# Bf16 three-part expert adds, one pair behind, and expert weights loaded by halves of the partitions

## The reference

```python
comb = jnp.sum(jax.nn.one_hot(eid, N_EXPERTS, dtype=F32) * (gw[:, None] * top_p)[..., None], axis=1)
a = jnp.einsum("nd,edf->nef", hf, w_gate)
u = jnp.einsum("nd,edf->nef", hf, w_up)
hid = jax.nn.silu(a) * u * comb[..., None].astype(h.dtype)
return jnp.einsum("nef,efd->nd", hid, w_down).reshape(B, T, D)
```

## Time and profile before

| | us |
|---|---|
| median of 3 runs | 1246.7 (1243.45 to 1247.94) |
| the profiled execution, its own time | 1241.49 |
| its span | 1239.8 |
| PE busy | 1141.6 (92%) |
| DVE busy | 470.2 (38%) |
| ACT busy | 233.4 (19%) |
| expert stage, layer 0 | about 347 to 629 |
| expert stage, layer 1 | about 928 to 1224 |

### The profile page before, as it was taken

The page is one execution under the profiler, slowest core; times in us unless marked ns, Lnnn a source line. Parts: engine busy times, 40 slices in busy tenths (PEclk is TensorE's granted clock), DMA queues, the critical chain, the costliest instruction groups (busy, mean ns, idle before and its releaser), DMA issues.

```text
span 1239.8 us, 13174 instructions
## 1 busy us (share of the span) xinstructions
PE 1141.6 (92%) x4522; PEld 491.0 (40%) x4522; DVE 470.2 (38%) x1089; ACT 233.4 (19%) x433; POOL 95.8 (8%) x163
## 2 busy tenths in 40 slices
PE   4899999999689999999959999999969999999984
PEld 0444444445333333333334554544633333333332
DVE  0453232336722333333364232235672333333335
ACT  0523220302310000000024233332330000000003
POOL 4000000004210000000040000001320000000000
PEclk8999999999799999999979999999779999999998
DMA  9966548427959999999650421212656999999962
GB/s 376 382 255 257 201 190 345 186 113 271 389 183 415 379 385 393 380 383 385 250 204 35 153 79 66 94 42 77 228 197 268 407 379 382 385 387 383 390 229 90
DMA packets 51241, 328.32 MB, mean 265 GB/s; under 512 B 6145, under 2 KB 8785, under 8 KB 14465
## 3 DMA queue, kind: packets, MB, share of 16 engines
q1 hardware_dynamic: 44672, 299.92, 61.5%
q0 software_dynamic: 4912, 20.95, 4.5%
q10 hardware_dynamic: 1616, 6.93, 1.5%
HBM read 320.90 MB, written 6.88 MB: 264 GB/s over the span
## 4 chain that ended last, share of the span: by engine, by line
PE 82%; DMA 8%; DVE 5%; ACT 2%; issue 2%; SPq 1%; DVEq 0%; ACTq 0%; PEldq 0%
PE bank L654 35%; PE bank L1029 17%; PE bank L1055 13%; PE bank L1046 9%; DMA ring<-in_w_moe 3%; PE bank L675 3%; DMA ring<-in_w_mod 2%; DMA ring<-in_w_out 1%; PE bank L1038 1%; PE bank L1071 1%; DMA ring<-in_w_in 1%; DMA region<-h_store,toki 1%; PE bank L1091 1%; PE bank L1012 1%; ACT hT L1410 1%
## 5 line engine op out<-in xcount | busy, mean ns | idle before, releaser
L1029 PE MATMUL bank<-ring,region 128*64 128x512 f32 x1024 | 237.6, 608 | 5.9 <-issue 5.9
L1055 PE MATMUL bank<-region 128*128 128x512 f32 x384 | 173.3, 601 | 0.0
L654 PE MATMUL bank<-ring,hT 128*128 128x512 f32 x384 | 171.6, 599 | 1.6 <-DMA ring<-in_w_in 1.6
L1029 PEld LDWEIGHTS bank<-ring,region 128*64 128x64 f32 x1024 | 70.2, 138 | 148.1 <-issue 148.1
L1046 PE MATMUL bank<-ring,region 128*64 128x512 f32 x512 | 115.8, 594 | 4.9 <-DMA ring<-in_w_moe 2.9
L1055 PEld LDWEIGHTS bank<-region 128*128 128x128 f32 x384 | 70.3, 190 | 102.5 <-issue 102.5
L654 PEld LDWEIGHTS bank<-ring,hT 128*128 128x128 f32 x384 | 70.9, 190 | 90.4 <-issue 90.2
L2079 DVE TENSOR_TENSOR region<-bank,region 128x512 f32<-128x512 f32 x128 | 82.4, 686 | 42.8 <-PE bank L1046 42.8
L654 PE MATMUL bank<-ring,region 128*128 128x512 f32 x192 | 86.4, 599 | 4.4 <-ACT region L1506 1.6
L654 PE MATMUL bank<-hT,ring 128*128 128x384 f32 x256 | 89.2, 500 | 1.1 <-DMA ring<-in_w_in 1.1
L2075 DVE TENSOR_TENSOR region<-region,bank 128x256 f32<-128x256 f32 x32 | 13.5, 422 | 200.9 <-ACT region L1535 200.9
(11 more groups left out here) (302 smaller groups left out, 970.3 us busy)
## 6 DMA issues: line engine op xcount, KB each, us to landing
ring<-in_w_moe SPq DMA_DIRECT2D x201, 1024.0 KB, 8.5
ring<-in_w_mod SPq DMA_DIRECT2D x48, 1024.0 KB, 9.7
ring<-in_w_in SPq DMA_DIRECT2D x24, 1024.0 KB, 8.2
ring<-in_w_out SPq DMA_DIRECT2D x4, 1024.0 KB, 7.3
ring<-in_w_out SPq DMA_DIRECT2D x8, 512.0 KB, 6.9
region<-gate_store POOLq DMA_DIRECT2D x4, 1024.0 KB, 6.6
region<-in_lnrows POOLq DMA_DIRECT2D x4, 1024.0 KB, 8.5
h_store<-region ACTq DMA_DIRECT2D x6, 512.0 KB, 3.0
```

What stands on the lines that cost most here:

```text
L654: ins = pe.matmul(out, lhsT, rhs, start=start, stop=stop, skip_group_check=True)
L1029: ins = pe.matmul(bank[6][u * CAP:(u + 1) * CAP, :], xs[:, k, u * CAP:(u + 1) * CAP], ring[:, u, j, at:at + 2 * DE], start=k == 0, stop=k ...
L1055: ins = pe.matmul(bank[2 * t + y][:, :], cwp[:, t * P:(t + 1) * P], ysb[:, min(t, 1), y * HALF:(y + 1) * HALF], start=False, stop=False, s ...
```

## The change

Four things are altered together.

1. **The add of the two latent blocks is in bf16, in three parts.** Every row has one token and thus one latent weight. `pair_weights` now also sums the latent part of `cwp` over the row into `wlat`; `gated` multiplies the latent copy by `wlat` and the gate row in one instruction; `cut_y` (DVE) and `cut_rows` (ACT) cut that f32 row into three bf16 rows, `hi`, `mid` and `lo`, by rounding and subtracting twice; `onehot` is a bf16 0/1 matrix out of `cwp > 0`. `add_parts` multiplies `onehot` by each of the three parts. The context block stays one f32 matmul with `cwc`, a copy of the context part of `cwp`.
2. **The add stands one pair behind.** In the loop PE runs up_first(i), turn(i-1), up_second(i), add(i-2), down(i-1); after the loop add(14) follows down(15), and add(15) is the old f32 `add_pair` on `ylast`. `cw_ready` is now given at the end of `cut_y`. 
3. **The halves of `down` change banks**: half 0 goes to bank 6 and half 1 to bank 7, and the wait for `hid_ready` of the next pair moves ahead of both. `up_first` waits for `ya_sb` instead of `yb_sb`, `turn_step` for `yb_sb` instead of `ya_sb`.
4. **The expert weights lie by partition in HBM and in the ring.** `w_moe` becomes (6, 128, 32 x 2048), the ring (128, 3, 2, 2048). `bring(i, y, j)` loads piece j of both experts of the pair for 64 of the 128 partitions, 16 KB in a row, so there are still two requests of 1 MB for a piece, and each consumer waits for both as before. In HBM the rows of one request are 256 KB apart. The last pair's down weights and the extra turns are still 128 partitions with 8 KB.

The core of the diff:

```diff
-                def bring(i, u, j):
-                    sp.dma_start(ring[:, u, j, :], A["w_moe"][bass.ds((l * NE + G * i + u) * 3 + j, 1)].rearrange("a p n -> p (a n)"))\
-                      .then_inc(landed[u][j], 16)
+                def bring(i, y, j):
+
+                    r = slice(y * P // 2, (y + 1) * P // 2)
+                    sp.dma_start(ring[r, j, :, :].rearrange("p g n -> p (g n)"), A["w_moe"][l * 3 + j, r, bass.ds(i * (G * PIECE), G * PIECE)])\
+                      .then_inc(landed[y][j], 16)
...
+            def add_parts(sig):
+
+                for y in range(2):
+                    c = slice(y * HALF, (y + 1) * HALF)
+                    for t in (1, 2):
+                        for part in (hi, mid, lo):
+                            pe.matmul(bank[2 * t + y][:, :], onehot[:, (t - 1) * P:t * P], part[:, c], start=False, stop=False, skip_group_check=True)
+                    ins = pe.matmul(bank[y][:, :], cwc, ysb[:, 0, c], start=False, stop=False, skip_group_check=True)
                 ins.then_inc(sig, 1)
...
                 up_first(1)
                 up_second(1)
-                add_step(0)
                 with pe.Fori(2, NPAIR) as i:
                     up_first(i)
                     turn_step(i - 1)
                     up_second(i)
+                    add_step(i - 2)
                     down_step(i - 1)
-                    add_step(i - 1)
...
-                down_step(NPAIR - 1, last=True)
-                add_step(NPAIR - 1, last=True)
+                down_step(NPAIR - 1, last=True)
+                add_step(NPAIR - 2)
+                add_pair((S["ya_sb"], S["yb_sb"]), NPAIR + p0, S["comb_done"])
...
+                def cut_rows(i):
...
+                    for y in range(2):
+                        c = slice(y * HALF, (y + 1) * HALF)
+                        act.wait_ge(S[("ya_sb", "yb_sb")[y]], i + (p0 + 1))
+                        f(hi[:, c], ysb[:, 1, c], ACT.Copy).then_inc(S["y_cut"], 1)
+                    for y in range(2):
+                        c = slice(y * HALF, (y + 1) * HALF)
+                        act.wait_ge(S["y_rest"], i * 2 + (2 * l * (NPAIR - 1) + y + 1))
+                        f(mid[:, c], ysb[:, 1, c], ACT.Copy).then_inc(S["y_cut"], 1)
...
+                def cut_y(i):
+                    c0 = l * (NPAIR - 1)
+                    dve.tensor_scalar(onehot, cwp[:, P:N], 0.0, None, ALU.is_gt)
+                    dve.tensor_copy(cwc, cwp[:, 0:P])
+                    for y in range(2):
+                        c = slice(y * HALF, (y + 1) * HALF)
+                        dve.wait_ge(S["y_cut"], i * 4 + (4 * c0 + y + 1))
+                        dve.tensor_tensor(ysb[:, 1, c], ysb[:, 1, c], hi[:, c], ALU.subtract).then_inc(S["y_rest"], 1)
+                    pair_weights(i + 1)
+                    for y in range(2):
+                        c = slice(y * HALF, (y + 1) * HALF)
+                        dve.wait_ge(S["y_cut"], i * 4 + (4 * c0 + y + 3))
+                        ins = dve.tensor_tensor(lo[:, c], ysb[:, 1, c], mid[:, c], ALU.subtract)
+                    ins.then_inc(S["cw_ready"], 1)
```

More of the change, by code:

```diff
@@ L333, in backbone_step @@
         xrows = [htok[:, t, :] for t in range(NT)] + [ysb[:, s, :] for s in range(2)] + [xlast]
+        bf = lambda a: a.bitcast(BF16)
+        hi, mid, lo = bf(htok[:, 0, 0:HALF]), bf(htok[:, 0, HALF:D]), bf(htok[:, 1, 0:HALF])
+        onehot = bf(htok[:, 1, HALF:HALF + N_LAT // 2])
+        cwc = htok[:, 1, HALF + P:HALF + 2 * P]
+        wlat = htok[:, 1, HALF + 2 * P:HALF + 2 * P + 1]
+        ylast = (xlast, htok[:, 2, :])
         xrow = [hT[0:MAXL, 2 + i, 0:MAXJ * NE].rearrange("p (a b) -> p a b", a=MAXJ) for i in range(5)]
@@ L1129, in down_step, with add_step @@
                             pe.wait_ge(landed[u][2], at(i))
-                    down(0, S["ya_ready"], 0 if last else 2)
                     if not (last or isinstance(i, int) and i == 0):
                         pe.wait_ge(S["hid_ready"], i + (p0 + 2))
+                    down(0, S["ya_ready"], 0 if last else 2)
                     down(1, S["yb_ready"], 0 if last else 2)
-                def add_step(i, last=False):
-                    pe.wait_ge(S["cw_ready"], i + (p0 + 1))
-                    add_pair((S["ya_sb"], S["yb_sb"]), i + (p0 + 1), S["comb_done"])
-                    if not last:
-                        pe.sem_inc(used[2], G)
+                def add_step(i):
+                    pe.wait_ge(S["cw_ready"], i + (l * (NPAIR - 1) + 1))
+                    add_parts(S["comb_done"])
+                    pe.sem_inc(used[2], G)
                 up_first(0)
@@ L2077, in gated @@
                 def gated(b, y):
-                    for s in (1, 0):
-                        ins = dve.tensor_tensor(ysb[:, s, y * HALF:(y + 1) * HALF], b, gate_row[:, s, y * HALF:(y + 1) * HALF], ALU.mult)
-                    return ins
+                    c = slice(y * HALF, (y + 1) * HALF)
+                    dve.scalar_tensor_tensor(out=ysb[:, 1, c], in0=b, scalar=wlat, in1=gate_row[:, 1, c], op0=ALU.mult, op1=ALU.mult)
+                    return dve.tensor_tensor(ysb[:, 0, c], b, gate_row[:, 0, c], ALU.mult)
@@ L2082, in keep_y @@
                 def keep_y(i):
+                    first = isinstance(i, int) and i == 0
+                    dve.wait_ge(S["cw_step"], i * 5 + 5 * (p0 + 1))
                     dve.wait_ge(S["ya_ready"], i + (p0 + 1))
-                    if not (isinstance(i, int) and p0 + i == 0):
+                    if not first:
                         dve.wait_ge(S["comb_done"], i + p0)
-                    gated(bank[7][:, :], 0).then_inc(S["ya_sb"], 1)
+                    gated(bank[6][:, :], 0).then_inc(S["ya_sb"], 1)
@@ L2090, in weights, with keep_last_y @@
+                def keep_last_y():
+                    for y, (got, done) in enumerate((("ya_ready", "ya_sb"), ("yb_ready", "yb_sb"))):
+                        c = slice(y * HALF, (y + 1) * HALF)
+                        dve.wait_ge(S[got], p0 + NPAIR)
+                        for s in (1, 0):
+                            ins = dve.tensor_tensor(ylast[s][:, c], bank[6 + y][:, :], gate_row[:, s, c], ALU.mult)
+                        ins.then_inc(S[done], 1)
                 def weights(col, step, done):
@@ L2100, in pair_weights @@
                 def pair_weights(i):
-                    if not (isinstance(i, int) and p0 + i == 0):
-                        dve.wait_ge(S["comb_done"], i + p0)
-                    weights(colq[:, bass.ds(i, 1)], S["cw_step"], i * 3 + 3 * p0).then_inc(S["cw_ready"], 1)
+                    done = i * 5 + 5 * p0
+                    weights(colq[:, bass.ds(i, 1)], S["cw_step"], done).then_inc(S["cw_step"], 1)
+                    dve.wait_ge(S["cw_step"], done + 4)
+                    dve.tensor_reduce(wlat, cwp[:, P:N], AX, ALU.add).then_inc(S["cw_step"], 1)
                 dve.wait_ge(S["xg_ready"], l + 1)
```

63 lines of the change are left out of this document (35 added, 28 removed).

## The result

The changed kernel takes 1653.68 us (median of 4, 1641.71 to 1654.98) against 1247.32 (1243.45 to 1250.43) for the kernel before: a ratio of 1.3261, with a 95% interval of 1.3226 to 1.3297. The profiled execution took 1653.11 us, its span is 1651.4. I had given 1237 with a range of 1230 to 1285, so the forecast was wrong; of the rivals, the whole of rival 2 (half the partitions as a narrow door, 1615, a chance of 0.14) came true.

What follows compares the result with a forecast made beforehand. The loop was taken as PE-bound with at most 1.5 us of DMA room a pair. Per layer -2.4 - 12 x (16.32 - 15.6) + 6.5 = -4.5 us, two layers -9 from 1246.7: 1237 us, range 1230 to 1285.

Steps and rivals of the forecast that it cites:

- rival 2: Expert-weight requests filling 64 partitions fall toward 212 GB/s: 29.7 us a pair, near 1615 us; chance 0.14 for the whole.
- The rate of requests: Expert-weight loads in the loop: shrunken windows still fit, 403 GB/s at 15.6 us a pair; bounds 425 and 212.
- a part of the loss: Engines partly colliding on half-partition requests, for example 350 GB/s and 18.0 us a pair: 1260 to 1330 us, chance 0.10.
- The adds: PE's add in the expert loop: bf16 matmuls take half an f32 instruction's time, 4.46 us a pair instead of 5.35.
- rival 3: A bf16 matmul in the add is no shorter than an f32 instruction: 18.1 us a pair, 1297 us; chance 0.04.
- PE's work and the pair: Expert loop: 15.43 us of PE work a pair, taken as 15.6 with request jitter, from 16.32; ends 15.43 and 16.0.
- DVE: DVE's chain from the end of down to cw_ready: 7.0 us, done 0.5 us before PE reaches the add at 7.5.
- Rival 4: DVE is late, 8 us to cw_ready: 15.9 us a pair, 1244 us; chance 0.22 shared with the request-rate rival.
- Ahead of the loop: First pairs of a layer: add(0) leaves, request landings pace the ups, next up_first comes 2.4 us earlier.
- Behind the loop: From the end of up_second(15) to the last add: 25.0 us instead of 18.5, so 6.5 lost a layer.
- The stages outside: Stages outside the experts run the same instructions, so no time was put on them.
- The sum: Each layer: -2.4 ahead, 12 turns shortened from 16.32 to 15.6, +6.5 behind, -4.5 us; two layers -9 us.

Runs made afterwards that it cites:

- adds_only: Kernel before with only the adds changed, its requests and HBM layout kept: 1249.97 us, ratio 1.0038 to the kernel before.
- full128_rows8k: Changed kernel with its new HBM layout, each request bringing one expert on all 128 partitions in 8 KB rows: 1246.78 us, ratio 1.0014 to the kernel before.
- one_2mb_rows16k: Changed kernel with one 2 MB request per piece, both experts on 128 partitions in 16 KB rows: 1247.35 us, ratio 1.0030 to the kernel before.
- early_requests: full128_rows8k with the first requests of a layer asked for slot by slot, as in the kernel before: 1244.38 us, ratio 0.9993.
- middle_half: Changed kernel with each piece cut into one 1 MB request for partitions 32 to 95 and two of 0.5 MB for the rest: 1536.8 us.

## Why the prediction was wrong, step by step

**The rate of requests: the step that failed.** The sum's pair of 15.6 us stands on 403 GB/s, and the runs showed 215. The prediction took its rate terms of 392 to 425 GB/s from rows on 128 partitions, and wrote beside them that no row shows whether 64 partitions are slower. The forecast then carried the good end, with the queue's depth as its reason ("engines have room to be at different requests"). That reason was worth nothing: the rate was 215 with 19.6 us from a request to its landing, and 222 with two queues. Why the halves do not overlap, no run shows. The other end of the same sentence, 212, was right to 1.5%. Rival 2's working gave a pair of 29.7 us, measured 29.34, and 165 us a layer for the 12 turns and the ends, with some 20 more for the pairs at both ends, 185; measured 192.7 and 192.4. The other 27 us of the 412, the 22.0 and 4.6 that lie ahead of the pairs, it left out: above all the gather, from 9.10 to 27.39 us. The Trainium skill's rule in SBUF — State Buffer, "Door 1: The DMA port swizzle", gives 64 partitions 196 GB/s at 1 MiB and about 218 as the limit (215 measured here). It was the only evidence on the very operation that the change introduces, and it got 0.14, with 0.10 more for a part of the loss. Where the trace is silent on an operation and a rule speaks, the silence is no counterweight.

The rest of the steps can be judged in adds_only and full128_rows8k, where the rate is whole. One turn of adds_only:

```profile
399.86 3.63 PE bank L1037 x16
403.49 0.37 PE bank L1046 x2
403.86 3.58 PE bank L1037 x16
407.44 1.40 PE bank L1073 x6
408.84 0.86 PE bank L1074 x2
409.70 1.29 PE bank L1073 x6
411.00 0.86 PE bank L1074 x2
411.85 3.58 PE bank L1054 x16
415.44 3.63 PE bank L1037 x16
```

**The adds: right.** 1.40 + 0.86 + 1.29 + 0.86 = 4.41 us, predicted 4.46. Six bf16 matmuls take 1.29 to 1.40 us, 0.215 to 0.233 each, and two f32 instructions 0.43 each. Half the time for bf16 was right, and rival 3 falls.

**PE's work and the pair: nearly right.** A turn without a wait is 15.58 us (399.86 to 415.44), predicted 15.43. Twelve turns, 399.86 to 589.61, average 15.81, with three waits for the ring in the chain; I had taken 15.6 and kept 16.0 as the other end. At 6.29 MB that is 398 GB/s, against the 403 that I took. Nor was the loop before quite "PE alone", as I read it from one pair. Its chain goes once through the ring in layer 0, and its twelve turns (393.56 to 589.90) average 16.36 us, not 16.32:

```profile
421.61 12.27 DMA ring<-in_w_moe
```


**DVE: right.** The last operations ahead of cw_ready in adds_only, with the end of down at 446.63:

```profile
446.70 0.75 DVE L2113 SCALAR_TENSOR_TENSOR region<-bank,region 128x512 f32<-128x512 f32 x1 [0.31 <-PE bank L1054]
...
448.29 1.29 DVE L2133 TENSOR_TENSOR region<-region 128x512 f32<-128x512 f32 x2
...
451.46 0.42 DVE L2164 TENSOR_REDUCE region<-region 128x1 f32<-128x256 f32 x1
451.79 1.28 DVE L2138 TENSOR_TENSOR region<-region 128x512 bf16<-128x512 f32 x2
```

It is done at 453.07, 6.4 us behind the end of down (predicted 7.0), and PE comes to the add at 454.17, 7.5 behind (7.5). Rival 4 falls.

**Ahead of the loop: too good.** From the start of up_first(1) to where the 12 whole turns begin, the chain of adds_only has 371.06 to 399.86, 28.80 us; before it was 363.32 to 393.56, 30.24. That is 1.4 won instead of 2.4 (in layer 1, 1.6). The ring landed as worked out, 7.0 us after its request (7.7), but PE had waited, and up_first(2) then took 5.35 us at a granted clock of 0.68, where I had taken 3.58:

```profile
375.43 7.00 DMA ring<-in_w_moe
...
382.56 5.35 PE bank L1037 x16
```

**Behind the loop: right in layer 1, 3 us short in layer 0.** Predicted 25.0 us for 18.5 before; measured 28.1 in layer 0 (597.19 to 625.27) and 25.2 in layer 1 (1181.75 to 1206.91). The chain of adds_only there, first layer 0:

```profile
605.24 0.75 DVE region L2113
...
606.92 1.22 DVE region L2133 x2
...
608.82 0.25 ACT region L1556
...
609.11 6.58 PE bank L1054 x16
615.70 1.40 PE bank L1073 x6
```

and layer 1:

```profile
1181.75 1.40 PE bank L1073 x6
...
1193.67 3.65 PE bank L1054 x16
...
1201.74 5.17 PE bank L1063 x12
```

One wait was mis-read in both layers. Down(14) ended at 605.21, and down(15) began 3.9 us later, where I had 2.15 (5.8 less the 3.65 of down). ACT's copy of the hidden rows (L1556), which it waits for, stands on ACT behind the cuts of pair 14, and these wait for DVE's subtractions (L2133). I had named what stands behind the new waits on PE and SP, not on ACT. It cost little, because it took the place of the wait for cw_ready that I had put behind down(15): in layer 1 add(14) began 7.5 us behind down(14), for 7.1. The 3 us of layer 0 are the clock: down(15) took 6.58 us there at a granted clock of 0.55, and 3.65 in layer 1 at 1.00. The waits just ahead of it were the same in both (1.50 and 2.02 us), so why only one came out at the lower clock is not shown.

**The stages outside: not unchanged.** The gather of token rows took 11.42 us in layer 0 of adds_only, since the first expert requests had moved into it: 2.3 us that no term of mine held. In layer 1, where no expert weights move beside the gather, nothing was lost: from the routing (L1981, now L2014) to the first up it took 28.6 us before and 28.2 in adds_only.

**The sum, made again with these.** From the first up to the end of the last add adds_only takes 271.4 us in layer 0 and 267.4 in layer 1, against 268.9 and 270.0 before. That is 2.5 us slower and 2.6 faster, where I had 4.5 faster in each:

| us against before | forecast | layer 0 | layer 1 |
|---|---|---|---|
| pair 0, and the ups of turn 15 | 0 | +0.9 | -1.1 |
| ahead of the loop | -2.4 | -1.4 | -1.6 |
| twelve turns | -8.6 | -6.6 | -6.5 |
| behind the loop | +6.5 | +9.6 | +6.6 |

The pairs of both layers thus come out even, not 9 us faster. The span of adds_only is 8.5 us longer than that of before (1248.3 against 1239.8), and this lies outside the pairs: 6.9 us ahead of the first up of layer 0, of which the gather is 2.3 and 4.4 come before the routing, and 1.9 between the layers. I have no cause for the 4.4. The same point comes 1.4 us late in one_2mb_rows16k and 5.2 in early_requests, and the profiled execution of before was a quick one, 5.2 us under its median. The medians are the safer measure: the adds cost 0.38% (0.16 to 0.61%). So even without the narrow door the forecast of 9 us faster was wrong: its turns were too good by 2 us a layer, the piece ahead by 1, the one behind by 3 in one layer, and it put the stages outside at nothing.

## What to carry to other kernels

Look at which partitions a request reaches, not only at its bytes and rows: 64 rows in one half of the partitions went at 215 GB/s, 64 rows spread over both at 396, and neither a second queue nor shorter rows nor a queue that was always full gave the difference back. A loop change that takes work out of every turn and puts one step behind has to be charged for its ends; here 6.6 us won in the turns of a layer stood against 6.6 to 9.6 lost behind them, and the kernel with repaired ends is the one where the idea paid, 0.75%. Hold such a sum against the trace stage by stage and layer by layer: in adds_only the pairs of the two layers came out 2.5 us slower and 2.6 faster, while the whole span grew by 8.5 elsewhere. When a change introduces a kind of operation that the trace does not have, and a written rule prices it, give the rule the larger part of the chance.

## What the runs showed of the hardware

- Requests into partitions 0 to 63 and 64 to 127 in turn moved 215 GB/s (16 KB rows) and 224 (8 KB rows), at a DMA share of 1.01 to 1.02; over even and odd partitions 396; over all 128 395 to 400, in requests of 1 MB and of 2 MB, at a share of 0.97 to 0.98.
- Two queues, one for each half, moved 222 GB/s together. What holds them apart is not shown.
- The distance of rows in HBM (256 KB) cost nothing that can be measured: with the same adds, 1.0014 (0.9983 to 1.0045) of before with it and 1.0038 (1.0016 to 1.0061) without it.
- The same requests of middle_half went at 225 GB/s in layer 0 and at 277 in layer 1, for a reason that stays open.
- Requests that share the DMA engines with the gather of token rows in layer 0 stretch it: 9.10 us before, 11.42 in adds_only, 27.39 in the kernel after. In layer 1, without them, it took 4.96 us in the kernel after.
- The same eight f32 matmuls of down(15), behind the same two waits, took 3.65 us at a granted clock of 1.00 and 6.58 at 0.55 in two layers of one execution.
